# Products of constants in TensorE's pauses between time mixing and cross attention of a hybrid decoder block

## What is computed

```python
kk = heads(k * k_k)
kk = kk / jnp.maximum(jnp.linalg.norm(kk, axis=-1, keepdims=True), 1e-12)
k = k * (1.0 + (a - 1.0) * k_a)
...
def step(state, inp):            # scan over the 512 tokens
    ...
out = (out - mean) * lax.rsqrt(var + GN_EPS) ... * lnx_w + lnx_b
bonus = (jnp.sum(rh * kh * r_k, axis=-1, keepdims=True) * vh).reshape(b, s, w_)
return (out + bonus) * g, v_first
...
gates = sigmoid(proj_gates + gate_b)
branches = jnp.einsum("bsnc,ncd->bsnd", ys, branch_proj)
merged = jnp.einsum("bsnd,bsnd->bsd", gates, branches)
h = h + merged @ w_mix_out
h = h + memory_cross_attention(rms_norm(h, norm_ca), rms_norm(mem, norm_mem), ...)
```

## Time and profile before

| | before |
|---|---|
| median of 3 runs | 2297.96 us (2297.16 to 2303.62) |
| the profiled execution, its own time | 2292.51 us |
| its span in the profile | 2290.7 us |
| TensorE matmul busy | 2126.0 us (93%) |
| VectorE busy | 1101.4 us (48%) |
| ScalarE busy | 813.8 us (36%) |
| mean granted TensorE clock | 0.957 |

### The profile page before, as it was taken

The page is one execution under the profiler, slowest core; times in us unless marked ns, Lnnn a source line. Parts: engine busy times, 40 slices in busy tenths (PEclk is TensorE's granted clock), DMA queues, the critical chain, the costliest instruction groups (busy, mean ns, idle before and its releaser), DMA issues. The chain is left out here.

```text
span 2290.7 us, 30020 instructions
## 1 busy us (share of the span) xinstructions
PE 2126.0 (93%) x12032; PEld 1686.6 (74%) x12032; DVE 1101.4 (48%) x1737; ACT 813.8 (36%) x1271; POOL 103.5 (5%) x134
## 2 busy tenths in 40 slices
PE   6999785997999899799999999999999899999997
PEld 5888551784888787688888877886566578888886
DVE  4553227445544353447777334313666655432433
ACT  3112653223323242334444213223455544422331
POOL 0000000660000000000000001000000000000000
PEclk9999796997999999899999998988999999999998
DMA  4323000000332233022323233320111122233322
GB/s 148 101 92 103 21 1 0 3 3 1 94 102 93 99 113 120 19 83 101 99 93 106 100 137 118 99 74 19 37 39 38 38 83 87 97 98 96 100 93 83
DMA packets 47853, 173.54 MB, mean 76 GB/s; under 512 B 5144, under 2 KB 7448, under 8 KB 47488
## 3 DMA queue, kind: packets, MB, share of 16 engines
q1 hardware_dynamic: 45440, 162.99, 21.7%
q0 software_dynamic: 1728, 8.23, 1.1%
q10 hardware_dynamic: 576, 0.84, 0.1%
HBM read 169.90 MB, written 2.13 MB: 75 GB/s over the span
## 5 line engine op out<-in xcount | busy, mean ns | idle before, releaser
L198 DVE TENSOR_TENSOR weights_lo<-weights_raw,weights_hi 128x1024 fp32r<-128x1024 f32 (+2 forms) x288 | 363.6, 1263 | 802.9 <-ACT weights_hi L190 802.7
L190 ACT ACTIVATE weights_hi<-weights_raw 128x1024 fp32r<-128x1024 f32 (+2 forms) x288 | 313.5, 1088 | 875.1 <-PE end_ps L223 245.6
L221 PE MATMUL sp_ps<-arena_parts,weights_hi 128*128 128x512 f32 x720 | 283.6, 394 | 10.8 <-DVE arena_parts L282 10.3
L223 PE MATMUL sp_ps<-arena_parts,weights_lo 128*128 128x512 f32 x720 | 281.6, 391 | 0.0
L222 PE MATMUL sp_ps<-arena_parts,weights_hi 128*128 128x512 f32 x720 | 281.6, 391 | 0.0
L221 PE MATMUL end_ps<-arena_parts,weights_hi 128*128 128x512 f32 x576 | 224.8, 390 | 2.2 <-DVE arena_parts L2723 1.7
L223 PE MATMUL end_ps<-arena_parts,weights_lo 128*128 128x512 f32 x576 | 224.1, 389 | 0.0
L222 PE MATMUL end_ps<-arena_parts,weights_hi 128*128 128x512 f32 x576 | 224.1, 389 | 0.0
L221 PEld LDWEIGHTS sp_ps<-arena_parts,weights_hi 128*128 128x128 f32 x720 | 136.3, 189 | 41.1 <-issue 12.0
L222 PEld LDWEIGHTS sp_ps<-arena_parts,weights_hi 128*128 128x128 f32 x720 | 136.3, 189 | 28.7 <-issue 0.7
L223 PEld LDWEIGHTS sp_ps<-arena_parts,weights_lo 128*128 128x128 f32 x720 | 136.0, 189 | 28.6
(11 more groups left out here) (392 smaller groups left out, 3514.5 us busy)
## 6 DMA issues: line engine op xcount, KB each, us to landing
weights_raw<-w_up SPq DMA_DIRECT2D x44, 512.0 KB, 3.4
weights_raw<-w_proj SPq DMA_DIRECT2D x38, 512.0 KB, 3.4
weights_raw<-w_gates SPq DMA_DIRECT2D x32, 576.0 KB, 3.7
weights_raw<-w_ca SPq DMA_DIRECT2D x32, 512.0 KB, 3.4
weights_raw<-w_down SPq DMA_DIRECT2D x16, 704.0 KB, 4.1
weights_raw<-w_in SPq DMA_DIRECT2D x22, 512.0 KB, 3.4
weights_raw<-w_logits SPq DMA_DIRECT2D x16, 512.0 KB, 3.5
weights_raw<-w_ff1a SPq DMA_DIRECT2D x16, 512.0 KB, 3.4
```

The lines of the kernel that those rows point to most:

```text
L190: act.activation(self.w_hi[:, g % 2, 0:cols], self.raw[:, g % 2, 0:cols], ACT.Copy).then_inc(self.hi_ready, 1)
L198: dve.tensor_tensor(self.w_lo[:, g % 2, 0:cols], self.raw[:, g % 2, 0:cols], self.w_hi[:, g % 2, 0:cols].bitcast(F32), ALU.subtract).then_ ...
L221: pe.matmul(out, left[0], right[0], start=start, stop=False)
L223: return pe.matmul(out, left[1], right[0], start=False, stop=stop)
```

## The change

`idle_products(core, pe, bank, n)` issues n float32 products of two constants, a 128x128 block of ones and a 128x512 mask, into a PSUM bank that nothing reads. It is called at seven places, 57 products in all: 6 at the end of time_mix_stage, 12 in time_mix_scale_stage before the wait for k_made, 5 and 12 in time_mix_out_stage, 7 at the end of gates_stage, 3 at the end of mix_stage and 12 in clear_semaphores_stage. Two PSUM tensors grow by one bank, and the clear stage gets one. In time_mix_stage the two last loops of VectorE change places, and TensorE waits for the first product of the bonus before it writes into bank 0.

```diff
 def clear_semaphores_stage(core):
-    with core.nc.Block() as block:
-        @block.sync
-        def _(sp):
-            for sem in core.stage_sems:
-                sp.sem_clear(sem)
+    with core.nc.psum_tensor("idle_ps", [P, T], F32) as ps:
+        with core.nc.Block() as block:
+            @block.sync
+            def _(sp):
+                for sem in core.stage_sems:
+                    sp.sem_clear(sem)
+            @block.tensor
+            def _(pe):
+                idle_products(core, pe, ps[:, :], 12)
...
+def idle_products(core, pe, bank, n):
+    for _ in range(n):
+        pe.matmul(bank, core.c("ones"), core.c("causal4"), start=True, stop=True)
...
 # time_mix_stage
+    bonus_taken = core.sem("tm_bonus_taken")
...
                 for c in range(NW):
                     pe.matmul(ps[:, (2, 3, 6, 7)[c], :], spread[:, c * P:(c + 1) * P], norm, start=True, stop=True).then_inc(norm_spread, 1)
+                pe.wait_ge(bonus_taken, 1)
+                idle_products(core, pe, ps[:, 0, :], 6)
...
                 for c in range(NW):
+                    dve.wait_ge(bonus_sum, c + 1)
+                    dve.tensor_tensor(bonus[:, c, :], ps[:, (0, 1, 4, 5)[c], :], v[:, c, :], ALU.mult).then_inc(bonus_taken, 1)
+                for c in range(NW):
                     dve.wait_ge(norm_spread, c + 1)
                     dve.tensor_tensor(kk[:, c, :], kk[:, c, :], ps[:, (2, 3, 6, 7)[c], :], ALU.mult)
-                for c in range(NW):
-                    dve.wait_ge(bonus_sum, c + 1)
-                    dve.tensor_tensor(bonus[:, c, :], ps[:, (0, 1, 4, 5)[c], :], v[:, c, :], ALU.mult)
...
 # time_mix_scale_stage
                     if n == 4:
+                        idle_products(core, pe, ps[:, 7, :], 12)
                         pe.wait_ge(k_made, NW)
...
 # time_mix_out_stage
                 mm.then_inc(var_done, 1)
+                idle_products(core, pe, ps[:, 5, :], 5)
                 pe.wait_ge(spread_in, 16)
                 pe.wait_ge(inverted, 1)
                 for c in range(NW):
                     pe.matmul(ps[:, c, :], spread[:, c * P:(c + 1) * P], rstd, start=True, stop=True).then_inc(rstd_spread, 1)
+                idle_products(core, pe, ps[:, 5, :], 12)
...
 # gates_stage
-        ps = ctx.enter_context(nc.psum_tensor("gt_ps", [P, 6, T], F32))
+        ps = ctx.enter_context(nc.psum_tensor("gt_ps", [P, 7, T], F32))
...
                 core.used += 32
+                idle_products(core, pe, ps[:, 6, :], 7)
...
 # mix_stage
-        ps = ctx.enter_context(nc.psum_tensor("mix_ps", [P, 4, T], F32))
+        ps = ctx.enter_context(nc.psum_tensor("mix_ps", [P, 5, T], F32))
...
                 mix.tensor(pe)
+                idle_products(core, pe, ps[:, 4, :], 3)
```

## The result

| | before | after |
|---|---|---|
| median | 2297.12 us (20 runs, 2293.42 to 2303.62) | 2304.52 us (20 runs, 2293.6 to 2311.04) |
| ratio | | 1.0027 [1.0016, 1.0038] |
| profiled execution: own time, span | 2292.51, 2290.7 us | 2306.83, 2305.0 us |
| mean granted clock | 0.957 | 0.964 |

The account below looks back on a forecast made before the run. TensorE bounds the kernel, through its clock and the pauses between stages. 11.7 us of overrun at three meetings against 8 us of faster work summed to +3.8 us, taken as +3 on the median 2297.96: 2301 us, range 2291 to 2308.

Parts of the forecast that it names:

- 1: Changed loop order in time mixing: no effect, as VectorE's 4.9 us stay its own.
- Part 2: Six products at the end of time mixing end after VectorE and delay the scaling stage: +3.3 us (+2.6 to +4.0).
- Part 3: Twelve products in the scaling stage end 4.0 us before k_made, hidden; clock falls again: -0.3 us (-0.5 to 0).
- Parts 4 and 5: Output stage: five products after the variances hidden; twelve after the spread overrun VectorE's chain: +5.5 us (+3.5 to +6.3).
- Parts 6 and 7: Gates start at the high clock: -2.3 us; seven products ending the gates are hidden, mix starts high: -1.9 us.
- Part 8: Three products ending the mix are hidden; cross projections start faster unless one-column sums lower the clock: -2.0 us (-3.3 to -0.5).
- Part 9: Twelve clear-stage products delay ScalarE: +2.9 us; the clock stays up for the work behind: -1.4 us (-2.6 to -1.2).
- A meeting that does not wait: Rival: stage-end meetings pass while queued products are in flight, sum -3.5 us, 2294.5 us; chance 0.15.
- Eight-row and one-column work that holds the clock: Rival: narrow work begun at the high clock keeps it there (spread, sums), sum +0.5 us, 2298.5 us; chance 0.08.
- Constants that do not lift the clock: Rival: moving ones and zeros counts as no work, so meetings overrun at the low clock: 2325 to 2340 us; chance 0.05.

Follow-up runs that it names:

- e4_order_only: Changed kernel with all 57 constant products left out; loop order, semaphore and larger PSUM tensors stay: 2296.47 us, 0.9997 of before.
- e8_no_six: Changed kernel without its six products at the end of time mixing: 2301.47 us, 1.0014 of before.
- e2_hidden_only: Changed kernel without the six in time mixing, the twelve after the spread and the twelve in the clear stage: 2295.11 us, 0.9988 of before.
- e3_fitted: Changed kernel with no products ending time mixing, five instead of twelve after the spread, eight instead of twelve in the clear stage: 2286.03 us, 0.996 of before.
- e9_fitted_no_clear: e3_fitted without its eight clear-stage products, so counts 0, 12, 5, 5, 7, 3, 0: 2287.09 us, 0.9942 of before.
- e7: Changed kernel without its twelve products after the eight-row spread: 2302.07 us, 1.0015 of before.
- e5_clear_24: Changed kernel with 24 instead of 12 products in the clear stage: 2316.72 us (two runs), 1.0085 of before.
- e6_clear_8_rows: Changed kernel with the clear stage's twelve products using 8 rows of the constants instead of 128: 2307.99 us (five runs), 1.0044 of before.
- e1: Changed kernel without its twelve products in the clear stage: 2300.62 us, 1.0008 of before.
- e10: e3_fitted without its five products after the spread, so counts 0, 12, 5, 0, 7, 3, 8: 2293.93 us, 0.9978 of before.
- e11: e9_fitted_no_clear with four instead of three products at the end of the mix: 2285.44 us, 0.9947 of before.
- e12: The kernel of e9_fitted_no_clear once more on another chip: 2283.23 us, 0.9943 of before.

## Why the prediction was right, point by point

The terms, in the times of the two profiled executions:

| part | stretch (before, after) | forecast | measured |
|---|---|---|---|
| 1 | order alone (e4_order_only) | 0 | -0.7 ± 2.2 |
| 2 | first of VectorE's eight last products to first turn: 5.17, 8.01 | +3.3 | +2.8 |
| 3 | first turn to first chunk record: 22.50, 22.62 | -0.3 | +0.1 |
| 4, 5 | first mean to gates' first split: 24.97, 30.81 | +5.5 | +5.8 |
| 6 | that split to the mix: 207.34, 205.06 | -2.3 | -2.3 |
| 7 | mix to the one-column sums: 49.71, 47.80 | -1.9 | -1.9 |
| 8 | sums to first score of cross attention: 105.02, 102.76 | -2.0 | -2.3 |
| 9 | last copy to split: 8.72, 11.83 | +2.9 | +3.1 |
| 9 | first weights record to first residual add: 9.50, 8.02 | -1.4 | -1.5 |
| | sum | +3.8 | +4.0 |

The measured sum is made of the unrounded differences. Its closeness to the forecast is in part luck, since it takes one execution for before. e4_order_only does the same work, and its trace has the same stretches for parts 2, 6 and 7, within 0.03 us for 3 to 5, but 105.45 us for part 8 and 10.27 for the second half of part 9; against it the parts add up to +2.7. The stretches between these, which the change does not touch, differ by 0.3 us at most up to middle_region; ahead of part 2 the profiled execution of after was 2.1 us early (376.56 against 378.62).

*Prices of a product.* The gates' seven took 6.17 us and the clear stage's twelve 10.54: 0.86 us each behind the tail of 0.17, as forecast.

*Part 2.* The rise came 3.2 us after the first product (forecast 4.1), inside the bounds, which is the missing half microsecond. (The prediction's own numbers, 386.7 and 383.49, give 3.2 and not 3.3.) In e8_no_six the term is gone from the trace, and the runs move by 3.0 us ± 3.9 with it.

*Part 3.* The twelve ended 3.91 us before k_made (forecast 4.0) and the clock fell as the turns began, at 400.9, so that nothing was won. e8_no_six shows what the prediction named as the alternative: with a short pause the clock holds under the turns. That wins nothing either, which the prediction didn't see: the clock falls in the chunks, and from the first turn to the first mean it takes 151.5 us before, 151.3 after and 151.4 to 151.5 in e8_no_six, e2_hidden_only, e3_fitted and e9_fitted_no_clear. So these twelve products gain 0.2 us at most in any trace; no kernel was run that leaves out only them. The Trainium skill (TensorE: Matmul & The Clock Gate, Part 4: PE-mode transpose) has transposes not count as work for the clock; here it rose 3.5 us into transposes (400.72, back at 404.2), and 32 of them at 1.00 in e8_no_six did not lower it, so the runs disagree, at least for these float32 turns.

*Parts 4 and 5.* The largest term was right in its mechanism: the clock fell 4.0 us behind the start of the spread, and dense work with all rows brought it back in 3.4 us. Confirmed from both sides: without the twelve the stage is 6.2 us shorter (e7), and with five of them the gain at the gates is had for nothing (e9).

*Parts 6 and 7.* As forecast; the cover of the seven held: VectorE ends the gates at 771.05, 0.6 us behind them.

*Part 8.* The clock fell under the sums, and the forecast, which put its value between "falls" and "holds", happened to match. Its bound was too narrow: from the sums to cross attention it took 100.3 us in e9_fitted_no_clear, where the clock held, so -4.7 and not -3.3. The prediction took VectorE's pace for the limit of the 256-column products; e9_fitted_no_clear has 28 records in 3.40 us where before had 27 in 5.50. Cross attention gives a part back: from its first score to its last copy it takes 35.2 us there and 34.3 in after, with a low stretch of 6.8 us in it instead of 3.4.

*Part 9.* Both halves as forecast in the profile, net +1.6 us. Over all runs, taking the twelve out gave 4.4 us, and doubling them cost 13 us for 10.3. Both intervals hold the profile's figure, both middles lie above it. For the doubled ones the clock may be the rest: the two executions of e5_clear_24 were at the low level for 167 and 171 us, the median of after is 161 (worked out as below), and 8 us at half rate are 4.

*The median.* The sum forecast was +3.8, the median +3; measured were +6.2 (3.7 to 8.7). The step that was off is the last one, from the profiled execution to the median: the prediction took 0.8 us off for longer low stretches in a usual run. One such is seen (e4_order_only needs 0.8 us more than before in the second half of part 9), but nothing was set for the untouched 1300 us behind these stages. From the first residual add of middle_region to the end of the span they took 1314.6 us before (2290.7 - 976.08) and 1327.1 after (2305.0 - 977.90), and in the twelve experiments 1315.1 to 1325.5, with no code changed in them. Of the 12.5 us, 9.4 are in the paired attention (251.8 us before and 261.2 after, from the first product into pa_ps to the first into end_ps). The longest low stretch there, in before and in after:

```profile
1580.80:1587.40 6.60, 6.60 (x19) 3.21 (x16) 4.96 (x13) 1.97 (x8) 0.00 (x0) 0.50 0.00 0
1585.40:1606.00 20.60, 20.60 (x60) 11.29 (x61) 10.76 (x26) 5.54 (x18) 0.00 (x0) 0.50 0.00 1
```

TensorE is busy throughout both, and 14 us more at half rate are 7 us. So one profile against one says 14 us where the runs say 6. What separates the executions is time at the low level. It can be worked out for each one, to some 2 us, as twice its span times one less its mean clock: 142 us for the fastest of after's twenty (2293.60 us) and 176 for the slowest (2311.04), 34 us apart, and half of that is the 17.4 us between them. By the same sum the two profiled executions have 198 us (before) and 167 (after), 31 less; the medians are 204 to 211 (the four sets of executions of before beside the experiments) and 161 (after), at least 43 less. The 12 us or more between these differences, at half rate, are 6 us or more of the 8 by which the profiles and the runs disagree. Whether the products upstream shift how long the clock is low behind them, or it is chance, stays open; it may well be the some 2 us that the runs have above the sum. The same holds for the best version: from its first turn to the first weights record behind the clear stage its trace has 574.5 us (381.89 to 956.35) where before has 582.8 (383.79 to 966.58), -8.3, and its runs have -13.

*The three rivals.* A meeting that does not wait: refuted by e5_clear_24. Eight-row and one-column work that holds the clock: refuted for eight rows by after (fall at 554.5) and e6_clear_8_rows. For one column it is mixed: in the traces the clock fell 1.1 to 1.4 us into the sums in after, e1, e2, e5, e6, e7, e8 and e10, and held in e3, e9, e11 and e12. Ahead of the sums stand the same three products and a pause of 1.40 or 1.41 us in all but e11 (four products, 0.54 us). All four in which it held have five products behind the spread, 250 us earlier, which is no mechanism; with one trace each it may differ from execution to execution, and what decides there, the sums or the pause, is open. Constants that do not lift the clock: refuted by the groups of parts 2 and 5 and by e9_fitted_no_clear, 3.0 to 3.4 us at the low level and then the rise.

## What to carry to other kernels

Work put into an engine's pause is free only up to the moment at which the slowest other engine is done. At a meeting of all engines each further product costs its full 0.86 us here, and all it can return is the low-clock stretch behind it, 1.5 to 2.3 us. So take from the timeline how many products the cover holds and stop there (32 of them: -13 us; 57: +6 us). And look whether the clock is still high where the work is: the twelve covered products in the scaling stage gained 0.2 us at most, as the clock fell in the turns or in the chunks behind them. Before the last pause ahead of dense work, look at what kind of work leads up to it: after narrow products the first 3 us of filler only buy the clock back. Sum the terms from the traces, but get the size of a total of a few microseconds from many runs, because stages that nobody touched moved by 12 us between single profiles.

## What the runs showed of the hardware that was not expected

- Products with 8 rows let the granted clock fall though TensorE was busy without a break: 3.7 us into them at the clear stage, and then 13.5 us at 0.50 (e6_clear_8_rows, one trace). Before the change it could only be seen that such work does not raise it. The Trainium skill (TensorE: Matmul & The Clock Gate, Part 1: The HAM clock gate) lets the clock follow how busy TensorE has been; by that it should have stayed up.
- After eight full products and a pause of 2.2 us the clock was high at the next product and fell 1.3 us into dense work of all rows (e3_fitted), to come back at 963.0. The same was seen after the spread, where it fell at 554.6 with full products running since 554.12 (after). A high level at the first product is thus no promise for the next microseconds.
- Under sixteen sums of one column, behind a pause of 1.4 us (0.54 us in e11_mix_4), the clock fell in the traces of eight kernels and held in those of four runs, though the kernels are alike around them.
